# A hybrid recurrence and pooling block on one core: three projections cut into pieces of 272, 384 and 384 columns instead of 348, 346 and 346

## The reference, cut to what matters

```
L = 16 meta tokens + 1024 tokens = 1040
h = rms_norm(z)                                    # 1040 x 1024
p = h @ w_in + b_in                                # 1040 x 8192: q, f, v, g, u, g_pool, m_hg, m_pool
log_f = log(lb + (1 - lb) * sigmoid(f));  k = (1 - lb) * sigmoid(-f)
o = gated linear recurrence over (q, k, v, log_f)  # 8 heads of 128, chunk by chunk
y_hg   = (rms_norm(o) * silu(g)) @ w_down_hg
pooled = trailing mean of u over 2, 4, 8 or 16 tokens, minus u itself
y_pool = ((pooled @ pool_w) * scale * silu(g_pool)) @ w_down_pool
z = z + (sigmoid(m_hg) * y_hg + sigmoid(m_pool) * y_pool) @ w_out
out = rms_norm(z)[16:]
```

## Time and profile before

| | before |
|---|---|
| median of 3 runs | 1184.43 us (1184.26 to 1184.43) |
| span of the profiled execution, first to last instruction | 1182.9 us |
| time of the runs beyond that span | about 1.5 us |
| PE busy | 1168.8 us, 99% of the span |
| DVE, ACT, POOL busy | 49%, 27%, 7% |
| granted TensorE clock | 0.998 on average |

### The profile page before, as it was taken

One profiled execution on the slowest core, in us unless ns is written; L12 is line 12 of the kernel. 1 busy time (PEld: TensorE's weight loads), 2 busy tenths in 40 slices (PEclk: granted clock), 3 DMA queues, 4 the chain that ended last, 5 costly groups with the idle time before them and its releaser, 6 DMA issues. The chain is left out here.

```text
span 1182.9 us, 17065 instructions
## 1 busy us (share of the span) xinstructions
PE 1168.8 (99%) x6700; PEld 1019.1 (86%) x6700; DVE 583.2 (49%) x948; ACT 316.2 (27%) x550; POOL 78.1 (7%) x135
## 2 busy tenths in 40 slices
PE   8999999999999999999999999999999999999996
PEld 8998989898989989888888888889889898888885
DVE  6464847574756747464311111114466566656233
ACT  7422223132223132222221221212322322122122
POOL 2200000000000000000010000000000000211111
PEclk9999999999999999999999999999999999999999
DMA  6111110011111001122222112212111111446123
GB/s 223 48 37 36 37 36 33 21 35 35 35 35 35 31 24 33 35 72 72 71 89 72 71 70 72 71 71 70 38 62 36 44 53 42 154 142 229 56 98 116
DMA packets 22288, 78.16 MB, mean 66 GB/s; under 512 B 3280, under 2 KB 3280, under 8 KB 22256
## 3 DMA queue, kind: packets, MB, share of 16 engines
q1 hardware_dynamic: 15008, 54.60, 13.4%
q0 software_dynamic: 6960, 22.59, 5.6%
q10 hardware_dynamic: 288, 0.53, 0.2%
HBM read 65.13 MB, written 12.58 MB: 66 GB/s over the span
## 5 line engine op out<-in xcount | busy, mean ns | idle before, releaser
L745 PE MATMUL acc<-h_hi,w_hi 128*128 128x512 f32 (+4 forms) x1232 | 447.9, 364 | 0.7 <-DVE h_lo L1007 0.7
L745 PE MATMUL acc<-h_lo,w_hi 128*128 128x512 f32 (+4 forms) x1232 | 440.9, 358 | 0.0
L745 PE MATMUL acc<-h_hi,w_lo 128*128 128x512 f32 (+4 forms) x1232 | 439.5, 357 | 0.0
L745 PEld LDWEIGHTS acc<-h_hi,w_hi 128*128 128x128 f32 x1232 | 231.6, 188 | 29.4 <-DVE h_lo L1007 0.9
L745 PEld LDWEIGHTS acc<-h_hi,w_lo 128*128 128x128 f32 x1232 | 231.8, 188 | 27.4
L745 PEld LDWEIGHTS acc<-h_lo,w_hi 128*128 128x128 f32 x1232 | 231.6, 188 | 26.2
L1018 DVE TENSOR_TENSOR w_lo<-raw,w_hi 128x1024 fp32r<-128x1024 f32 x80 | 97.7, 1221 | 177.3 <-ACT w_hi L454 177.3
L745 PE MATMUL acc<-a_hi,w_hi 128*128 128x512 f32 x256 | 99.6, 389 | 0.0
L745 PE MATMUL acc<-a_lo,w_hi 128*128 128x512 f32 x256 | 99.6, 389 | 0.0
L745 PE MATMUL acc<-a_hi,w_lo 128*128 128x512 f32 x256 | 99.6, 389 | 0.0
L454 ACT ACTIVATE w_hi<-raw 128x1024 fp32r<-128x1024 f32 x80 | 84.2, 1052 | 11.9 <-DMA part_spill<-part 3.8
(11 more groups left out here) (179 smaller groups left out, 1396.7 us busy)
## 6 DMA issues: line engine op xcount, KB each, us to landing
raw<-in_wstream SPq DMA_DIRECT2D x88, 512.0 KB, 3.3
xin<-in_x SPq DMA_DIRECT2D x8, 512.0 KB, 3.6
smp_spill<-gm POOLq DMA_DIRECT2D x16, 256.0 KB, 2.3
part_spill<-part POOLq DMA_DIRECT2D x16, 256.0 KB, 2.3
sp_in<-smp_spill POOLq DMA_DIRECT2D x16, 256.0 KB, 3.0
pt_in<-part_spill POOLq DMA_DIRECT2D x16, 256.0 KB, 3.8
xr<-in_x POOLq DMA_DIRECT2D x16, 256.0 KB, 3.3
out_z<-row SPq DMA_DIRECT2D x8, 512.0 KB, 3.7
```

The source lines that it names most:

```text
L745: ins = pe.matmul(out_ap, a, b, start=first and n == 0, stop=final and n == 2)
```

## The change

One line, the table `WITH_META`, changes. Each entry is the first column and the number of columns.

```
-WITH_META = ((0, 348), (348, 346), (694, 346))
+WITH_META = ((0, 272), (272, 384), (656, 384))
```

## The result

The changed kernel takes 1189.16 us (median of 5 runs, 1189.09 to 1189.37), the kernel before 1184.41 (5 runs). That is 4.75 us more, a ratio of 1.0041 with a 95% interval of 1.0029 to 1.0054. The forecast was 1188.6, slower by 4.2 us.

The account below looks back on a forecast made before the run. TensorE, busy 99% of the span, was taken to bound the kernel. Terms -0.3 + 3.8 + 0.15 + 0.6 = +4.2 us on the 1182.9 us span, plus 1.5 us for the median, gave 1188.6 us; range 1186.6 to 1190.6.

Parts of the forecast that it names:

- Step 0 comes before its input: Head bodies 2 to 7: TensorE reaches step 0 before VectorE's `prepared` is ready, losing 0.63 us a body, 3.8 us.
- The columns: All 22 blocks: matmuls of 384 columns cost what the line through 348 and 512 gives, changing the total by -0.3 us.
- The bounds, 171.6 and 178.4: Lowest and highest ns for a 384-column matmul, moving the columns' sum by -3.4 to +3.8 us.
- What is late next: VectorE's chain from step 0 to step 2 slips, delaying step 2 by 0.1 us a body, 0.6 us; bounds 0 and 1.2.
- The slip at `gated_o`: VectorE's `gated_o` waits for `o_transposes`, which come 0.19 us later; middle value taken, 0.1 us a body.
- my sign that it would come 0.3 us or more behind the last load: At step 2, the weight load of L808 should come 0.3 us or more behind the load before it.
- Body 1: Step 0 of body 1 waits for `v_copied`, a stall of 0.1 to 0.4 us, taken as 0.15.
- TensorE's queue absorbs the stall: Rival at step 0: the stall costs TensorE nothing, only -0.3 us is left, 1184.1 us; 6 in 100.
- pieces beginning at a multiple of 16 columns are cheaper: Rival on 384-column pieces: aligned starts cost 171.6 ns, giving 1185.5 us, 8 in 100; under 168.2 ns, 2 in 100.
- the rival of growing stalls: Full 0.19 us at `gated_o`, 0.4 us in body 1, 384 columns at some 176.5 ns: 1191.3 us; 12 in 100.
- The limit of 173.1 ns: Time of a 384-column matmul from which down the cheaper aligned pieces can't be told from no change.
- the second rival: Pieces of 384 columns with aligned starts are cheaper, 171.6 ns, gaining 3.4 us: 1185.5 us; 8 in 100.

Follow-up runs that it names:

- experiment 3: Changed kernel with VectorE's prepare of the next head moved ahead of the last gate: 1185.63 us; the same move with the widths of the kernel before: 1184.34 us.
- (2): The changed kernel's widths in the other order, 384, 384 and 272 columns, in all 22 blocks: 1184.75 us, ratio 1.0003 to the kernel before.
- (4): Kernel before with all 22 blocks in other widths: 304, 368 and 368 columns took 1185.27 us; 336, 352 and 352 took 1184.18 us.
- experiment 5: Kernel before with pieces of 304, 368 and 368 and prepare ahead of the last gate: 1183.07 us; also with value blocks 368, 368, 304: 1182.61 us.

## Why the prediction was right, step by step

**Step 0 comes before its input: right, in mechanism and size.** Forecast were a wait for L1080 in six bodies, 0.67 us at the load, 0.05 given back because the second load follows the first in 0.11 us behind a stall and not in 0.16. Measured: six, 0.66 us, named by the waits. Moving the input (experiment 3) takes it away but for 0.13 us, turning the order (2) takes it away wholly, and it has the threshold that the slack before implied (4). In body 2 the wait was 0.72 us, so the mean less the 0.05 is 0.62, and six times 0.62 is 3.7 us of the 4.9 in the span.

**The columns: the sign was wrong, the size small.** The line between 348 and 512 columns gave 174.8 ns for 384; it took 176.0. With 22 x 48 matmuls this is 1.3 us, and the term is 22 x 0.04 = +0.9 us where -0.3 was forecast. The step that failed is the assumption that the cost is a line in the width. Experiment 4 shows that it fails on the other side too: 304 columns take 138.0 ns where the line has 139.2. At 368 it holds, with 167.6 against 167.7. The bounds, 171.6 and 178.4, held.

**What is late next: a mis-sized term.** The slip at `gated_o` was forecast at 0.1 us a body and is there: L1244 comes 0.70 behind L1137, before some 0.6 (319.07 with L1137 at 318.48 in that timeline). What the forecast had left open, the way from the end of the transposes to the instruction, is 0.21 us (320.22 + 1.03 = 321.25, and L1244 at 321.46), so of the 0.31 before some 0.1 was slack. VectorE's chain to step 2 grew by 0.09. The step that failed is that such a slip was priced as lost to TensorE in full. L1129 now begins 2.09 us behind the load of step 0 and not 2.13, since the second load follows the first faster behind the stall, so the distance from step 0 to step 2 grew by 0.05 in body 5 and by 0.03 in the mean of the six bodies. TensorE's own columns on that way grew by about as much. The load of step 2 waits 0.28 - 0.13 = 0.15 us, before 0.12, and my sign that it would come 0.3 us or more behind the last load did not appear: it is 0.28 as before. So this term is some 0.1 to 0.2 us in all and not 0.6. That it was near zero is not for want of a tight place: with the value and pool blocks alone changed, step 2 lost some 4 us.

**Body 1.** Forecast 0.15. In the changed kernel the last load ahead of step 0 is at 61.30 and that of step 0 at 61.56:

```profile
61.30 0.19 PEld L745 LDWEIGHTS acc<-h_hi,w_lo 128*128 128x128 f32 x1
61.56 0.30 PEld L804 LDWEIGHTS levels<-ek,kt 128*128 128x128 f32 x2
```

That is 0.13 over the beat, less the 0.05 of the faster loads behind it: 0.1. The input that decides is `v_copied`, as forecast: ScalarE's L542 ends at 61.20 + 0.25 = 61.45, 0.11 us ahead of the load, and L1080 at 61.28.

Together 3.7 + 0.9 + 0.15 + 0.1 = 4.85 us, against 4.9 in the span and 4.75 in the medians. Of the 4.9, 0.08 us lie ahead of the first body, where nothing was changed. That the forecast's 4.2 came so near is in part luck: one term was 1.2 too low and another 0.45 too high.

**The rivals.** That TensorE's queue absorbs the stall is refuted by the 0.66 us and by the time. That pieces beginning at a multiple of 16 columns are cheaper is not borne out for 384: 176.0 ns is 16.0 over its column time, above the 13.8 of 348. The table of 304, 368 and 368 is cheap and has such starts, but so has that of 336, 352 and 352, whose block takes 11.43 us, as before. Of the rival of growing stalls one part of three came about: 384 columns took 176.0 ns, near its 176.5. The full slip at step 2 and the 0.4 us in body 1 did not.

**Slips in the working.** The limit of 173.1 ns in the second rival is taken from +4.2, which holds the columns' -0.3 already; from the +4.5 that the same rival starts with it is 172.8. The columns' sum by the rows is -0.13 us, and -0.3 overstates it. VectorE does stand idle between level 0 and L1163, for 0.15 us at most at a time, at waits for its own instructions. None of these changes the outcome.

## What to carry to other kernels

Where one engine is busy all the time and its side work is spread between pieces of its main work, the widths of the pieces are a schedule. A cut that leaves their sum unchanged still moves every stage behind it, and what counts is each stage's arrival against its input, measured from what releases that input. So list for each waiting stage the slack in the trace (its weight load against the end of its input), mark those with under a microsecond, and check which distances the new cut shortens: step 0 here had 0.1 us and lost 0.8, while step 2 had none and was saved only because the forget and value blocks changed together. If a narrow piece has to be somewhere, put it behind the tight stages, or move the input ahead of whatever unrelated wait stands in front of it.

## What the runs showed that was not expected

The cost of a matmul beyond its columns at 2.4 GHz (the granted clock was 0.997 of it) is no smooth function of the width. In a pool group, from the starts of first matmuls, it is 11.3 ns at 304 columns, 12.5 at 272, 14.3 at 368, 13.8 at 348 and 16.0 at 384. It is no function of the width alone either. These are the first matmuls of three pieces and of the next block in the run with 336, 352 and 352:

```profile
844.45 0.31 PE L747 MATMUL acc<-h_hi,w_hi 128*128 128x336 f32 x1
...
848.15 0.32 PE L747 MATMUL acc<-h_hi,w_hi 128*128 128x352 f32 x1
...
851.99 0.33 PE L747 MATMUL acc<-h_hi,w_hi 128*128 128x352 f32 x1
...
855.88 0.31 PE L747 MATMUL acc<-h_hi,w_hi 128*128 128x336 f32 x1
```

The two pieces of 352 columns take 0.1600 and 0.1621 us a matmul. They differ in their first column, 336 and 688. Over the 22 blocks the table of 304, 368 and 368 was worth 1.3 us against that of 348, 346 and 346, both without a wait at step 0 (experiment 5). The cause is open.
